# Loading x in two halves, and moving the squares and the inverse norm, in the first stage of a decoder step

## What is computed

```
def rms_norm(x, g):
    xf = x.astype(jnp.float32)
    y = xf * lax.rsqrt(jnp.mean(xf * xf, axis=-1, keepdims=True) + EPS)
    return (y * g.astype(jnp.float32)).astype(x.dtype)
...
    n = rms_norm(x, norm_attn)
    q, k, v, qi, ki, wi, u = project(n, w_in, pos)
```

## Time and profile before

| | us |
|---|---|
| median of three executions | 2526.94 |
| lowest and highest of them | 2517.93, 2528.32 |
| the profiled execution | 2520.81 |
| its span in the trace | 2519.2 |
| TensorE busy in the span | 2468.1 |
| VectorE, ScalarE, POOL busy | 1186.3, 834.7, 383.2 |

### The profile page before, as it was taken

One profiled execution on the slowest core, in us unless ns is written; L12 is line 12 of the kernel. 1 busy time (PEld: TensorE's weight loads), 2 busy tenths in 40 slices (PEclk: granted clock), 3 DMA queues, 4 the chain that ended last, 5 costly groups with the idle time before them and its releaser, 6 DMA issues.

```text
span 2519.2 us, 49839 instructions
## 1 busy us (share of the span) xinstructions
PE 2468.1 (98%) x19410; PEld 2389.0 (95%) x19412; DVE 1186.3 (47%) x1796; ACT 834.7 (33%) x1091; POOL 383.2 (15%) x430
## 2 busy tenths in 40 slices
PE   7999999999989999999999999999999999999998
PEld 6968999996679999999999999999999999999998
DVE  6688989887433352333333332433233333333354
ACT  6153344326322243333223333223333222222233
POOL 2334899623610000000000000000000000000000
PEclk9999999999999999999999999999999999999999
DMA  7414233315864443232233222233322223232232
GB/s 247 122 38 115 73 83 84 88 43 177 277 194 108 119 109 92 83 92 65 87 108 89 86 85 72 86 99 92 92 83 81 75 85 108 86 88 84 68 91 95
DMA packets 424729, 255.07 MB, mean 101 GB/s; under 512 B 19980, under 2 KB 413444, under 8 KB 423969
## 3 DMA queue, kind: packets, MB, share of 16 engines
q1 hardware_dynamic: 412864, 224.91, 31.0%
q0 software_dynamic: 11792, 29.23, 3.6%
HBM read 243.66 MB, written 11.27 MB: 101 GB/s over the span
## 4 chain that ended last, share of the span: by engine, by line
PE 86%; issue 4%; POOL 3%; DVE 3%; ACT 2%; DMA 1%; SPq 0%; POOLq 0%; DVEq 0%; ACTq 0%
PE ps L1566 80%; POOL y L577 3%; PE ps L1829 1%; PE ps L1659 1%; PE ps L1803 1%; PE ps L1849 1%; ACT tap L762 1%; PE ps L1785 1%; DMA xN<-in_x_prompt 1%; PE ps L1878 0%; DMA stN<-in_state_conv 0%; POOL tapS L585 0%; PE ps L1942 0%; PE ps L1749 0%; PE ps L1742 0%
## 5 line engine op out<-in xcount | busy, mean ns | idle before, releaser
L987 DVE TENSOR_TENSOR wlo<-raw,whi 128x1024 fp32r<-128x1024 f32 (+1 forms) x366 | 447.9, 1225 | 1098.1 <-ACT whi L636 1084.7
L1566 PE MATMUL ps<-xhi,whi 128*128 128x272 f32 (+1 forms) x4512 | 935.4, 288 | 8.8 <-DVE xlo L995 2.8
L1566 PE MATMUL ps<-xhi,wlo 128*128 128x272 f32 (+1 forms) x4512 | 934.1, 288 | 0.0
L1566 PE MATMUL ps<-xlo,whi 128*128 128x272 f32 (+1 forms) x4512 | 930.3, 288 | 0.0
L636 ACT CAST whi<-raw 128x1024 fp32r<-128x1024 f32 (+1 forms) x410 | 429.0, 1048 | 1167.6 <-PE ps L1566 1090.2
L1566 PEld LDWEIGHTS ps<-xhi,whi 128*128 128x128 f32 (+1 forms) x4512 | 708.5, 188 | 12.5 <-issue 3.9
L1566 PEld LDWEIGHTS ps<-xlo,whi 128*128 128x128 f32 (+1 forms) x4512 | 708.4, 188 | 0.0
L1566 PEld LDWEIGHTS ps<-xhi,wlo 128*128 128x128 f32 (+1 forms) x4512 | 703.7, 189 | 0.0
L1566 PE MATMUL ps<-hidh,whi 128*128 128x272 f32 x1408 | 291.4, 288 | 0.0
L1566 PE MATMUL ps<-hidl,whi 128*128 128x272 f32 x1408 | 291.2, 288 | 0.0
L1566 PE MATMUL ps<-hidh,wlo 128*128 128x272 f32 x1408 | 291.1, 288 | 0.0
(11 more groups left out here) (314 smaller groups left out, 1551.4 us busy)
## 6 DMA issues: line engine op xcount, KB each, us to landing
raw<-in_w_gate SPq DMA_DIRECT2D x88, 512.0 KB, 3.7
raw<-in_w_up SPq DMA_DIRECT2D x88, 512.0 KB, 3.8
raw<-in_w_in SPq DMA_DIRECT2D x72, 512.0 KB, 3.8
raw<-in_w_down SPq DMA_DIRECT2D x64, 384.0 KB, 3.4
raw<-in_w_down SPq DMA_DIRECT2D x64, 320.0 KB, 3.2
raw<-in_w_out SPq DMA_DIRECT2D x32, 512.0 KB, 5.3
ring_pages<-in_cache_k SPq DMA_DIRECT2D x40, 128.0 KB, 3.6
ring_pages<-in_cache_k POOLq DMA_DIRECT2D x40, 128.0 KB, 3.5
```

Source lines behind the costliest of these rows:

```text
L987: ve.tensor_tensor(wlo[:, u.slot, :, 0:cols], raw[:, u.slot, :, 0:cols], whi[:, u.slot, :, 0:cols].bitcast(F32), ALU.subtract).then_inc(s_ ...
L1566: ins = te.matmul(ps[0:cols, 2 * slot + half, 0:HALF], w[:, u.slot, t, 0:cols], x[:, k0 + t, HALF * half:HALF * half + HALF], start=(hf == ...
```

## The change

x is loaded in two halves of the channels: five loads of the first 1024 channels, the first two units of weights, five loads of the second 1024, the next two units. SP no longer waits. New semaphores `s_xm` count the second halves. The squares become ten passes over half rows (five per half, the sums of the second half in columns 40 to 44 of `stat`), the first five after pieces 7, 8, 12, 15 and 17, the other five after the last xhi. VectorE adds the two sums, behind the low part of unit (-1, 6). The square root stands on ScalarE behind the rounding of that unit, the reciprocal and the diagonals behind the last xlo. TensorE turns seven pieces ahead, then three behind ki and two behind qi, and does the row sums and the constants' turn behind the fourth quarter instead of the third. ScalarE rounds units (-1, 6) and (-1, 7) before it copies the constants. POOL issues `tab` and the rest behind the second store of xT, once the fifth second half is there, and clears `qpad` later. `junk`, which the squares write, shrinks to half and moves.

```diff
             for hf in range(2):
+                for i in range(5):
+                    sp.dma_start(xN[i][0:tok[i], D // 2 * hf:D // 2 * hf + D // 2],
+                                 x_rows[i][:, D // 2 * hf:D // 2 * hf + D // 2]).then_inc((s_xn, s_xm)[hf][i], 16)
                 load(Unit(-1, 2 + 2 * hf), w_in[:, UK * hf:UK * hf + UK, COL_KI:COL_KI + KIW], cols=KIW)
                 load(Unit(-1, 3 + 2 * hf), col(w_in, COL_QI, hf))
...
-            nc.gpsimd.memset(qpad[:, :, :, :], 0.0).then_inc(s_pool, 1)
             nc.gpsimd.memset(stat[:, :], EPS).then_inc(s_pool, 1)
-            pool.wait_ge(s_xn[4], 16)
-            pool.dma_start(tab[:, :, :], a["c_rope"]).then_inc(s_const, 16)
...
             for kb in range(4):
+                if kb == 2:
+                    pool.wait_ge(s_xm[4], 16)
+                    pool.dma_start(tab[:, :, :], a["c_rope"]).then_inc(s_const, 16)
...
+            def squares(m):
+                hf, i = divmod(m, 5)
+                act.wait_ge((s_xn, s_xm)[hf][i], 16)
+                if m >= 1:
+                    act.wait_ge(s_ssq, m)
+                nc.scalar.activation(junk[0:tok[i], :], xN[i][0:tok[i], D // 2 * hf:D // 2 * hf + D // 2], ACT.Square,
+                                     accum_out=stat[0:tok[i], (8, 40)[hf] + i:(9, 41)[hf] + i]).then_inc(s_ssq, 1)
...
-                if n <= 2:
-                    squares(n)
-                if n in (6, 8):
-                    squares(n // 2)
-                if n == 9:
-                    act.wait_ge(s_ssq, 5)
-                    nc.scalar.activation(stat[:, 16:21], stat[:, 8:13], ACT.Sqrt, bias=stat[:, 0:1], scale=1.0 / D
-                                         ).then_inc(s_sqrt, 1)
+                if n in (7, 8, 12, 15, 17):
+                    squares((7, 8, 12, 15, 17).index(n))
...
             x_high(19)
+            for m in range(5, 10):
+                squares(m)
+            hi(Unit(-1, 6))
+            act.wait_ge(s_ssq, 11)
+            nc.scalar.activation(stat[:, 16:21], stat[:, 8:13], ACT.Sqrt, bias=stat[:, 0:1], scale=1.0 / D
+                                 ).then_inc(s_sqrt, 1)
+            hi(Unit(-1, 7))
             act.wait_ge(s_ct, 2)
...
-            for q in range(4, 6):
-                hi(Unit(-1, 2 + q))
...
             x_low(19)
+            lo(Unit(-1, 6))
+            dve.wait_ge(s_ssq, 10)
+            ve.tensor_tensor(stat[:, 8:13], stat[:, 8:13], stat[:, 40:45], ALU.add).then_inc(s_ssq, 1)
+            dve.wait_ge(s_sqrt, 1)
+            ch.link(ve.reciprocal(stat[:, 16:21], stat[:, 16:21]))
...
-            x_rows_turned(0, 9)
+            x_rows_turned(0, 7)
             pe.wait_ge(s_cc, 1)
             for kb in range(4):
                 hf, t0 = kb // 2, 4 * (kb % 2)
                 pe.wait_ge(s_xl, 5 * kb + 5)
                 unit(Unit(-1, 2 + 2 * hf), 1, hf, k0=UK * hf, cols=KIW, t0=t0, t1=t0 + 4)
-                x_rows_turned(9 + 5 * kb, 11 + 5 * kb)
+                x_rows_turned(7 + 5 * kb, 10 + 5 * kb)
                 unit(Unit(-1, 3 + 2 * hf), 0, hf, k0=UK * hf, t0=t0, t1=t0 + 4)
-                x_rows_turned(11 + 5 * kb, 14 + 5 * kb)
-                if kb == 2:
-                    pe.wait_ge(s_pool, 1)
-                    pe.wait_ge(s_rd, 5)
...
+                x_rows_turned(10 + 5 * kb, 12 + 5 * kb)
+            pe.wait_ge(s_pool, 1)
+            pe.wait_ge(s_rd, 5)
+            pe.wait_ge(s_xe, 20)
```

More of the change, by code:

```diff
@@ L253, in build @@
         s_xn = [sem(f"s_xn{i}") for i in range(5)]
+        s_xm = [sem(f"s_xm{i}") for i in range(5)]
         s_xt, s_xe, s_xg, s_xh, s_xl = sem("s_xt"), sem("s_xe"), sem("s_xg"), sem("s_xh"), sem("s_xl")
@@ L523, in _ @@
             nc.gpsimd.memset(ones[:, :], 1.0).then_inc(s_pool, 1)
-            nc.gpsimd.memset(qpad[:, :, :, :], 0.0).then_inc(s_pool, 1)
             nc.gpsimd.memset(stat[:, :], EPS).then_inc(s_pool, 1)
-            pool.wait_ge(s_xn[4], 16)
-            pool.dma_start(tab[:, :, :], a["c_rope"]).then_inc(s_const, 16)
-            for s in range(4):
-                pool.dma_start(rowselF[NS * s:NS * s + NS, :, :], a["c_rowsel"]).then_inc(s_const, 16)
-            pool.dma_start(causF[:, :], a["c_caus"]).then_inc(s_const, 16)
-            for kb in range(4):
+            for kb in range(4):
+                if kb == 2:
+                    pool.wait_ge(s_xm[4], 16)
+                    pool.dma_start(tab[:, :, :], a["c_rope"]).then_inc(s_const, 16)
+                    for s in range(4):
+                        pool.dma_start(rowselF[NS * s:NS * s + NS, :, :], a["c_rowsel"]).then_inc(s_const, 16)
+                    pool.dma_start(causF[:, :], a["c_caus"]).then_inc(s_const, 16)
                 pool.wait_ge(s_xe, 5 * (kb + 1))
@@ L535, in _ @@
             pool.wait_ge(s_xl, 20)
-            pool.wait_ge(s_ssq, 5)
+            pool.wait_ge(s_ssq, 11)
             pool.wait_ge(s_caus, 1)
             pool.wait_ge(s_ct, 2)
+            nc.gpsimd.memset(qpad[:, :, :, :], 0.0).then_inc(s_pool, 1)
             nc.gpsimd.memset(wsel[:, :, :, :], 0.0).then_inc(s_pool, 1)
@@ L636, in hi @@
                 nc.scalar.copy(whi[:, u.slot, :, 0:cols], raw[:, u.slot, :, 0:cols]).then_inc(s_hi, 1)
[L639 to L646, removed]
+            def squares(m):
[5 more added lines that the diff above has]
+                                     accum_out=stat[0:tok[i], (8, 40)[hf] + i:(9, 41)[hf] + i]).then_inc(s_ssq, 1)
+            act.wait_ge(s_pool, 2)
             act.wait_ge(s_ct, 1)
@@ L1012, in _ @@
                     lo(Unit(-1, 3))
[L1013 to L1018, removed]
                 if n == 10:
@@ L1022, in _ @@
             x_low(19)
+            lo(Unit(-1, 6))
[3 more added lines that the diff above has]
+            ch.link(ve.reciprocal(stat[:, 16:21], stat[:, 16:21]))
+            for t in range(5):
+                ve.tensor_scalar(diag[0:tok[t], t, 0:tok[t]], ident[0:tok[t], 0:tok[t]],
+                                 stat[0:tok[t], 16 + t:17 + t], None, ALU.mult).then_inc(s_rd, 1)
             dve.wait_ge(s_const, 16 * 11)
@@ L1591, in x_rows_turned @@
                     r = tok[i]
-                    if kb == 0:
-                        pe.wait_ge(s_xn[i], 16)
+                    if kb in (0, 2):
+                        pe.wait_ge((s_xn, s_xm)[kb // 2][i], 16)
                     if n >= 4:
@@ L1606, in _ @@
                 unit(Unit(-1, 2 + 2 * hf), 1, hf, k0=UK * hf, cols=KIW, t0=t0, t1=t0 + 4)
-                x_rows_turned(9 + 5 * kb, 11 + 5 * kb)
+                x_rows_turned(7 + 5 * kb, 10 + 5 * kb)
                 unit(Unit(-1, 3 + 2 * hf), 0, hf, k0=UK * hf, t0=t0, t1=t0 + 4)
-                x_rows_turned(11 + 5 * kb, 14 + 5 * kb)
-                if kb == 2:
-                    pe.wait_ge(s_pool, 1)
-                    pe.wait_ge(s_rd, 5)
[L1613 to L1622, removed]
+                x_rows_turned(10 + 5 * kb, 12 + 5 * kb)
+            pe.wait_ge(s_pool, 1)
+            pe.wait_ge(s_rd, 5)
+            pe.wait_ge(s_xe, 20)
+            for i in range(4):
+                te.matmul(ps[:, 6, P * i:P * i + P], ones[:, :], diag[:, i, :], start=True, stop=True)
+            te.matmul(ps[:, 7, 0:NS], ones[0:NS, :], diag[0:NS, 4, 0:NS], start=True, stop=True
+                      ).then_inc(s_sums, 1)
+            pe.wait_ge(s_const, 16 * 11)
+            te.transpose(ps[:, 4, 0:40], vecN[:, :], ident[0:40, 0:40])
+            for c in range(CT):
+                ins = te.transpose(ps[:, 5, CK * c:CK * c + CK], cwN[:, P * c:P * c + P], ident[0:CK, 0:CK])
+            ins.then_inc(s_ct, 1)
             tile(P_QI, 1)
```

6 lines of the change are left out of this document (1 added, 5 removed).

## The result

The changed kernel takes 2528.19 us (median of 20, 2524.61 to 2531.3) against 2522.58 us (20 runs of the kernel before, 2517.14 to 2528.32): 1.0020 times as long, interval 1.0012 to 1.0028, that is some 5 us slower, 3 to 7. A change within 0.5% was forecast, and that holds. The sum of +1.4 us doesn't, since the interval lies above it. The profiled execution of the changed kernel took 2528.5 us, span 2526.9.

The account below looks back on a forecast made before the run. It took the start of TensorE's unbroken matmul run as the bound: last ki 6.3 us sooner, against row sums +2.1, stall +3.1, kiraw +1.1, rope +1.1, restarts +0.3, together +1.4. That gave 2522.2 or 2528.3, taken as 2526, range 2514 to 2536.

Parts of the forecast that it names:

- The sum of +1.4 us: Start of the third tile, all terms added: 70.5 us against 69.1, with all later work moving with it.
- the tail: Work behind the last xhi: squares, weight rounding, low part, sum, root and diagonals; TensorE gets its row sums at 54.0 us.
- the stall: TensorE after the last qi: stands 3.1 us, from 50.9 to 54.0, waiting for the diagonals.
- Kiraw: Copy of ki that frees its accumulator, on ScalarE behind the two small constant copies: 1.1 us, uncovered.
- The rope: VectorE's last rope product, which frees the accumulator, ends at 70.3 to 70.4 us; TensorE waits 1.1 us.
- The second and third quarter of the ring: Time from ki to ki in the turn, copy, multiply, round, subtract sequence: 9.6 us, then 8.8 us.
- Rival D: Second-half weights land at 28 and 30 us, 2 us late; third ki slips 2.7 us: +4.1 us; chance 0.07.
- B, the hidden tail: Diagonals ready at 50.9 us, so the late norm work is covered: -3.5, at best -5 us; chance 0.22.
- the arrival of x: Half loads of x cost 1.6 us each by bytes, arriving at 5.4 to 10.7 us; first ki at 16.1.
- Rival E: A half load takes as long as a whole one: third tile at 83.2 us, +14 us; chance 0.04.
- the ring's first quarter: From first ki to second: 10.2 us, of which ki itself 3.1; second ki at 26.3 us.
- rival C: Idle TensorE falls to the slow clock at the row sums, doubling them: +2.1 us; chance 0.08.

Follow-up runs that it names:

- e5: Changed kernel with weight unit (-1, 6) rounded before the five late squares and kiraw copied before the two small constants; 2526.97 us, 1.0013 of the kernel before.
- e8: Changed kernel with 28 needless turns filling TensorE between the last qi and the wait for the diagonals; 2526.25 us, 1.0014 of the kernel before.
- e6: Changed kernel with nine squares where ScalarE stood idle, one after the last xhi, unit (-1, 6) behind the root; 2522.33 us, 1.0001 of the kernel before.
- e11: Changed kernel with nine pieces turned ahead, ten half squares spread over the ring, row sums before the fourth quarter; 2516.45 us, 0.9968 of the kernel before.
- e3: Changed kernel with eleven needless turns into an unused bank ahead of the first ki; 2525.85 us, 1.0008 of the kernel before.
- e2: Changed kernel with nine pieces turned ahead, then two behind ki and three behind qi, as before; 2520.97 us, 0.9986 of the kernel before.

## Why the prediction was right and wrong

**Right: the tail and what is late in it.** Five squares in a row, unit, root: the stall was forecast at 3.1 us and measured 2.98 and 2.96. Kiraw was forecast at 1.1 and measured 1.05. The rope as the next one late shows in e5 and e8 (0.39 and 0.80 us) once less of the slow clock covers it. The second and third quarter of the ring, forecast at 9.6 and 8.8 us, took 9.8 and 9.2. That the index pages' later start costs nothing fits what follows the third tile: 2450.1 us in both profiles before, 2450.1 (2526.9 - 76.8) and 2447.5 in those after. Rival D, late second weights, didn't come true: ScalarE's rounding of them at 29.44 us has no wait in front of it. Nor did B, the hidden tail; e6 and e11 are what it described, squares in ScalarE's gaps or inside the ring.

**Mis-sized: the arrival of x.** The step "half loads cost by bytes 1.6 us each: estimated arrivals 5.4, 7.1, 8.7, 10.3". In the two profiles of the changed kernel the turns began at 6.5 and 6.6, 7.8 and 7.9, 10.3 and 9.9, 12.5 and 11.6 us. The first half load comes only 0.6 us before a whole one did (7.07), so most of its time isn't bytes; the later ones are 1.3 to 2.5 us apart. The prediction's own sign of being wrong, more than 2.5 us apart, was just met in the first profile (7.80 to 10.32) and not in the second. Rival E, as long as a whole load, didn't come true. The first ki came at 17.5 to 18.4 us instead of 16.1: +1.4 to +2.3.

**Failed: the ring's first quarter.** The step "ki 3.1" in "From ki to ki the ring is now ... 10.2 us" took over the duration of a working TensorE, while seven pieces ahead instead of nine leave it idle for 2.4 us in front of that ki. It ran at half speed for most of its matmuls: 5.1 us. The quarter took 12.2 and 11.8 us in the two profiles. e3 gives 1.5 to 1.9 us back with needless work alone. The forecast had put the idle time's other cost in (piece 7 behind ki) but took it as given; e2, which turns nine ahead, takes 8.2 us for the same quarter and 2.5 less for the third.

**Failed: the chance of rival C.** It had 0.08 because the record grants 1.00 in the gaps of the first 51 us. It came true: 0.6 us in the sums and constants (2.7 instead of 2.1) and 2.3 us in the tile, 1.1 of it in place of the forecast wait for the rope. The rival's own price was wrong too: it doubled the sums (+2.1) and put nothing down for the tile. The Trainium skill, TensorE: Matmul & The Clock Gate, Part 1, says that an idle array falls to 1.2 GHz; this trace agrees at the second place with a granted clock of 0.50 after 2.98 us of idle time, at the first with durations in one profile and with the record in the other. How much idle time it takes the runs don't settle: the same 1.05 us was followed by the fall in e6 and not in e8.

The sum, third tile against before: forecast +1.4; loads +2.3 (first profile); slow first ki +2.0; rest of the ring +0.5; stall -0.1; sums and constants slow +0.6; tile slow +2.3; rope covered -1.1: +7.9, read +7.7. The second pair of profiles gives +6.8 (75.5 against 68.7), but their spans differ by only 4.2 us, because the changed kernel took 2.6 us less behind the third tile. The timed difference is 5 us (3 to 7). Over all profiles of all runs the part behind the third tile lasts 2446.7 to 2451.1 us; what moves it stays open. The timed runs of the kernel before reach 2528 to 2529 us, while its two profiled ones took 2520.8 and 2520.4; where its slower executions lose their time stays open.

**Failed: from the sum to the time.** The step "I take the middle of the two rounded up, 2526" mixed two figures for the kernel before, 2520.81 and 2526.94. So a forecast loss of 1.4 us became a time below the median that it would be measured against. Twenty runs later that median is 2522.58 and the changed kernel's 2528.19. That 2526 lies only 2 us off is luck: the edited stage lost some 5 to 6 us more than forecast, and the kernel before is 4.4 us faster than the three runs had it.

## What to carry to other kernels

A move that brings data sooner is worth what the engines that follow can take up: here 4 us won at the first matmul shrank to 1.4 us at the last one, because at the same time fewer pieces were turned ahead, so that ScalarE waited for them and TensorE stood idle, then ran slow. Before work is moved to the end of a chain, list everything that its engine has still to do behind the last useful step; ScalarE's five squares were cheaper inside a busy ring than behind it. And price a new idle stretch of TensorE twice, once for itself and once for the slow matmuls behind it; needless matmuls in the gap are a quick way to measure the second price.

## What the runs showed of the hardware that was not expected

The granted clock in the record was 1.00 while 24 matmuls took 5.1 us instead of 3.2. That isn't so in every profile. In all seven where the first ki was slow from its first matmul on, the record shows 1.00 there. In the two where it began at full speed and slowed down later, e8 and the changed kernel's second profile, the record shows 0.50 from 19 to 21 us. In e8 it slowed down only after its eighth matmul, behind the same 2.37 us of idle time, as TensorE's timeline has it:

```profile
17.67 0.45 PE L1568 MATMUL ps<-xhi,whi 128*80 128x272 f32 x2 [2.37 <-DVE wlo L988]
17.96 0.41 PE L1568 MATMUL ps<-xlo,whi 128*80 128x272 f32 x2
18.21 0.41 PE L1568 MATMUL ps<-xhi,wlo 128*80 128x272 f32 x2
18.46 0.47 PE L1568 MATMUL ps<-xhi,whi 128*80 128x272 f32 x2
18.73 0.65 PE L1568 MATMUL ps<-xlo,whi 128*80 128x272 f32 x2
19.18 0.66 PE L1568 MATMUL ps<-xhi,wlo 128*80 128x272 f32 x2
```

In e6 1.05 us of idle time behind the short matmuls was followed by a clock of 0.50, in e8 the same 1.05 us behind the 28 needless turns wasn't. The first half load of x landed 4.5 to 4.7 us after its issue where a whole one took 5.0 to 5.1.
